# The delta rule's block inverse in quarters of 32 columns instead of halves of 64

## The chip, the cores and the metric

One core of one Trainium2 chip runs the kernel. The metric is the device time of one execution in microseconds (us); lower is better. The kernel before has a median of 1058.83 us over three runs (1057.62 to 1060.48).

## The reference, cut to what matters

Two blocks of two layers each work on 256 rows of 1024 features, in float32. Block one has a gated delta rule of 8 heads beside an attention; its core is a unit lower triangular system for each chunk of the sequence:

```
lower = where(strict, (kb @ k.T) * decay, 0)
tmat  = eye + lower
u     = triangular_solve(tmat, v * beta)
w     = triangular_solve(tmat, kb * exp(gc))
```

The kernel takes chunks of 128 rows, works out the inverse of `tmat` explicitly, and multiplies by it. Block two (four attention branches, gated and merged) is not touched but for the order of its steps.

## The kernel before, in words

**Bulk work.** All projections stream their weights from HBM in units of 512 KB or less: SP issues a unit's load into one of five `raw` slots, ACT rounds it to `w_hi`, which has three slots (`split`, line 1362, through the helper on line 1347), POOL subtracts to get `w_lo` (lines 866 and 868), and TensorE multiplies hi by hi, hi by lo and lo by hi (lines 926, 934 and 941). These units are the `m` steps of the order, their loads and splits the `s` steps.

**Order.** Every engine walks one list, `PLAN`, and executes those of its steps that it has a handler for. The list comes from a string, `ORDER`: each letter takes the next step of its lane (`a` is the delta rule's chain of block one, `b` the attention, `m` the bulk matmuls, `s` loads and splits, and so on). So the string alone sets what stands before what in each engine's queue. Steps signal one another by semaphores. Chain steps on TensorE write the two `chain` buffers in PSUM in turn (`take`, line 951).

**The inverse.** It is done four times: two layers by two groups of four heads, each time for 8 matrices of 128 by 128 at once (4 heads by 2 row tiles). `sub` (DVE, line 1956) solves the 8 by 8 diagonal blocks and spreads them into `xth`, the transposed inverse: each partition holds the 64 columns of its own diagonal half, so that 8 matrices take 512 columns. `x1` (TensorE line 1055, drained by ACT line 1517) turns it into `xh`. Then four levels double the block size, 8 to 16, 32, 64 and 128. Of a level, `invY` multiplies the lower triangle's block with X (TensorE) and masks the product (DVE, line 1999), `invZ` multiplies by X from the other side, once for X and once for its transpose (TensorE, lines 1091 and 1092), and DVE subtracts the two (`invZ` line 2006, `invX` lines 2015 to 2019). On the first three levels and in `x1` each matmul takes a 64 by 64 block on one diagonal half of the array, and the two halves of a matrix follow one another (`half_blocks`, line 965; its matmul is line 970). The fourth level (lines 1080 and 1095) has 64 by 64 blocks that sit on one half only. Each float32 matmul is executed as two passes, so 16 matmuls are 32 records in the trace.

The order of the chain is written in `gdn_chain` (line 235): `sub`, `x1`, then `invY`, `invZ`, `invX` by level, with `vT` after the first level and `kT` in the last, then `kq`, `u`, `st`, `ks`, `o`.

Of the kernel before, what the change touches and what calls it, by code (L numbers as in the profile page):

```python
# [54 lines left out]
K_ID, K_TRIU, K_LEVEL, K_BLOCK, K_NEG, K_STR, K_NSTR, K_TRIL, K_ONE, K_FREQ, K_UNIT, K_LATER, K_HALF, K_OWN = (  # L55
    0, 128, 256, 448, 576, 832, 1088, 1344, 1472, 1600, 1640, 1648, 1776, 1777)
K_COLS = K_OWN + HALF


def shape_constants():  # L60
# [5 lines left out]
    own = HALF * (p // HALF) + f[:, 0:HALF]  # L66
    for n, s in enumerate(LEVELS[:-1]):
        c[:, K_LEVEL + n * HALF:K_LEVEL + (n + 1) * HALF] = (
            (p // (2 * s) == own // (2 * s)) & (p // s % 2 == 1) & (own // s % 2 == 0))
    c[:, K_BLOCK:K_BLOCK + P] = p // BLK == f // BLK  # L70
    c[:, K_OWN:K_OWN + HALF] = p // BLK == own // BLK
    c[:, K_UNIT:K_UNIT + BLK] = p % BLK == np.arange(BLK)[None, :]
    c[:, K_NEG + P:K_NEG + 2 * P] = np.where(f > p, np.float32(NEG), np.float32(0))
    c[:, K_STR:K_STR + P] = p < f
    c[:, K_STR + P:K_STR + 2 * P] = 1
# [159 lines left out]
def gdn_chain(g):  # L235
# [63 lines left out]
def lanes():  # L299
# [20 lines left out]
    "aaaaasammssvamsmssaamaaasaacsccasscccssammcmmsmaacssmmaacssccsmmmamaaasasmdabsmaaabssmmcsmaammassdbm"  # L320
    "adbmssaaammsssammsbadamsabaamamsaaaamssacmasccmaamasbsbbmacccscmammssmsccsaacbcmmbssmambbsaaasssammb"
    "bdsaaaamsssdmmmmaassdwbbssmmmsamcbmmamssssbbdbbmmaaambabxxsasbmaabbbsddmxssbaamswwamaaamaassmamsdwaa"
    "mwbasxsxmmsdmsaxbmwxsaxxxbmbbmxaxvsvsssmssmmmammsmaammsdsaaammsssssvammmmaaaascasscmmsccasscmcassccm"
    "msmaammcmsacsmcasmsassdaaaammasassmmaambbsmambacmaaamdassmssbdbssmaamabammaaamssaaadmsscamacsmssssaa"
    "mmamccacccmssbbscbcmmcamssacammbbsssmabbsmaaamdssaaaammssdsammadmmaabbscbbbmaswmmssdsbbbaassmsssmaaw"
    "maabmmbambsbxmxxbmssdbbbmmsssdamawammaasaadswwmbamasxxbsamaamssbaxdbbwxsxxmmmxxxsssssvsmmsvasadmmmmm"
    "mmsaaaasassaassmmdsssssdssbsdsbbmmmmmmsmmmmammmmsssaassdaasmmbbsaadbbsmmmbsaaasmmbddabbmbbmssaaamvba"
    "bmbsssddmmbbadmmsssybbmbssbmaambdsymsbamdsyyavbymbysydvvmmyssdmvssvvvvdmsvvvdmmmmssdymmmmmmvvvssssss"
    "yvvsmmmmmmmvmmmvsseeessvvvvaeeessmmaaammmbmmmmmmssdmssssssssdmmmmmadsasmsbaaammmbbbaassdasssdbbmbmma"
    "asaamsbmbsddbmbbmaaabmsssvbbmbasmmsabbdmbddsssasmabbssmymmambayddssmbsmbdsssydvyysmsdbsyyvvmmydmmmmv"  # L330
    "svsmdvvvvmsvvyssssmmvvvmmyvvmvvmssemmmmmsseemmvvvveemmme"
# [136 lines left out]
def build(nc, t, out):  # L468
    ctx = ExitStack()
    with ctx:  # L470
# [68 lines left out]
        xh, yh, xth = xx8[:, :, 0:HALF], yy8[:, :, 0:HALF], yy8[:, :, HALF:P]  # L539
        rhs = xx[:, 0, :, :].rearrange("p j n -> p (j n)")  # L540
# [335 lines left out]
        def _(pe):  # L876
            def handlers(p):
# [95 lines left out]

                def memT(r):
# [94 lines left out]
                def invY(g, n):  # L1069
# [6 lines left out]
                    if n < len(LEVELS) - 1:  # L1076
# [7 lines left out]
                def invZ(g, n):  # L1084
# [5 lines left out]
                    if n < len(LEVELS) - 1:  # L1090
# [242 lines left out]
        def _(act):  # L1333
# [15 lines left out]
            def handlers(p):  # L1349
# [167 lines left out]
                def x1(g):  # L1517
                    act.wait_ge(*p.after("tensor", "x1", g))
                    A(xh, heads(half("x1", g)[:, 0:R * 4 * HALF], R * 4), ACT.Copy).then_inc(p.done("x1"), 1)
# [121 lines left out]
                def ln_s(r):  # L1641
                    if r == 0:
# [6 lines left out]
                            stat=stat, avT=avT_, rn=rn, dec_b=dec_b, x1=x1, u=u_, st=st_, onorm_a=onorm_a, onorm=onorm, kinorm=kinorm, iT=iT,  # L1649
# [817 lines left out]
```

## Time and profile before

| | |
|---|---|
| median of 3 runs | 1058.83 us (1057.62 to 1060.48) |
| span of the profiled execution, first to last instruction | 1056.6 us |
| its own time | not listed apart from the span; the median is 2.2 us above the span |
| TensorE busy | 1025.6 us, 97% |
| DVE, ACT, POOL busy | 57%, 55%, 67% |
| granted TensorE clock, mean | 0.997 of full speed |

Busy time of TensorE is that in which at least one matmul is in flight. The chain that ended last says which engine the end of the execution hangs on from one moment to the next. A row of the timeline or of the chain of waits stands for a run of like instructions: its start, the time it takes, and how many there are.

### The profile page before, as it was taken

To read this page: it belongs to the slowest core of one execution; us is meant where nothing else is said; L and a number is where in the kernel's file an instruction comes from. 1 tells how busy PE (TensorE), PEld (TensorE's weight loads), DVE (VectorE), ACT (ScalarE), POOL (GpSimd) and SP (SyncE) were. 2 spreads that over 40 slices of the span, in tenths; PEclk is the share of its full clock that TensorE was granted. 3 is DMA by queue.
4 is the path that set the end of the run, shared out by engine and by line. 5 is a ranking of instruction groups with operands and counts; after the bars stand their busy time and mean duration, and the time that the engine had idled before them with its cause. 6 is when DMAs were issued, how large, how long until landed. Compare 5 with 4: busy or idle time off the path is not lost.

```text
span 1056.6 us, 18561 instructions
## 1 busy us (share of the span) xinstructions
PE 1025.6 (97%) x7112; PEld 886.4 (84%) x7112; DVE 599.0 (57%) x1181; ACT 577.4 (55%) x968; POOL 712.2 (67%) x550
## 2 busy tenths in 40 slices
PE   8999999999999999999999998999999989999986
PEld 8988998888877988899888887788888768888875
DVE  4774366786565557246584563517446560646564
ACT  4754347656644574336656744445576534567652
POOL 4786537872648787556766645897366978744794
PEclk9999999999999999999999999999999999999999
DMA  8664434653425555435444332665233546423451
GB/s 294 192 179 122 139 101 131 173 156 107 134 100 153 180 165 157 140 84 157 141 139 141 115 125 87 209 191 158 81 113 120 186 140 216 133 91 108 140 183 57
DMA packets 80584, 151.59 MB, mean 143 GB/s; under 512 B 6448, under 2 KB 12400, under 8 KB 80496
## 3 DMA queue, kind: packets, MB, share of 16 engines
q1 hardware_dynamic: 80496, 150.41, 46.9%
q8 instruction: 57, 0.93, 0.4%
q14 instruction: 31, 0.25, 0.1%
HBM read 149.34 MB, written 1.05 MB: 142 GB/s over the span
## 4 chain that ended last, share of the span: by engine, by line
PE 88%; DVE 4%; ACT 3%; POOL 3%; issue 2%; DMA 0%; POOLq 0%; SPq 0%; DVEq 0%; ACTq 0%
PE bulk L941 53%; PE bulk L926 12%; PE chain L962 5%; PE chain L970 4%; PE chain L1039 4%; PE chain L1307 1%; PE bulk L934 1%; PE chain L1288 1%; ACT arena L1347 1%; PE chain L1163 1%; PE chain L1179 1%; POOL w_lo L868 1%; DVE arena L1846 1%; PE chain L1030 1%; POOL w_lo L866 1%
## 5 line engine op out<-in xcount | busy, mean ns | idle before, releaser
L866 POOL TENSOR_TENSOR w_lo<-raw,w_hi 128x512 fp32r<-128x512 f32 (+3 forms) x259 | 340.7, 1316 | 292.4 <-ACT w_hi L1347 291.8
L868 POOL TENSOR_TENSOR w_lo<-raw,w_hi 128x512 fp32r<-128x512 f32 (+3 forms) x277 | 375.6, 1357 | 31.8 <-ACT w_hi L1347 31.8
L1347 ACT ACTIVATE w_hi<-raw 128x1024 fp32r<-128x1024 f32 (+4 forms) x277 | 277.3, 1019 | 210.1 <-PE bulk L941 163.4
L941 PE MATMUL bulk<-w_hi,hT_hi 128*128 128x512 f32 (+1 forms) x756 | 306.0, 405 | 0.8 <-ACT arena L1347 0.5
L941 PE MATMUL bulk<-w_hi,hT_lo 128*128 128x512 f32 (+1 forms) x756 | 294.4, 389 | 0.0
L941 PE MATMUL bulk<-w_lo,hT_hi 128*128 128x512 f32 (+1 forms) x756 | 204.2, 389 | 1.9 <-POOL w_lo L868 1.9
L941 PEld LDWEIGHTS bulk<-w_hi,hT_hi 128*128 128x128 f32 x756 | 142.4, 188 | 33.5 <-issue 1.9
L941 PEld LDWEIGHTS bulk<-w_lo,hT_hi 128*128 128x128 f32 x756 | 141.7, 188 | 32.7 <-POOL w_lo L868 3.4
L941 PEld LDWEIGHTS bulk<-w_hi,hT_lo 128*128 128x128 f32 x756 | 142.5, 188 | 26.8 <-issue 1.0
L926 PE MATMUL bulk<-hT_hi,w_hi 128*128 128x256 f32 x384 | 96.3, 289 | 0.0
L926 PE MATMUL bulk<-hT_lo,w_hi 128*128 128x256 f32 x384 | 94.0, 282 | 0.0
L962 PE MATMUL chain<-cst,arena 128*128 128x128 f32 (+1 forms) x544 | 73.4, 276 | 7.8 <-DVE arena L2223 3.5
L962 PEld LDWEIGHTS chain<-cst,arena 128*128 128x128 f32 (+1 forms) x544 | 62.7, 142 | 15.1 <-issue 9.3
L926 PEld LDWEIGHTS bulk<-hT_hi,w_hi 128*128 128x128 f32 x384 | 73.4, 191 | 0.9 <-ACT w_hi L1347 0.7
L1347 ACT ACTIVATE arena<-chain 128x512 f32<-128x512 f32 (+4 forms) x64 | 45.5, 727 | 52.0 <-PE chain L962 23.6
L926 PEld LDWEIGHTS bulk<-hT_lo,w_hi 128*128 128x128 f32 x384 | 73.5, 191 | 0.0
L1846 DVE SCALAR_TENSOR_TENSOR arena<-bulk,par,arena 128x253 f32<-128x253 f32 (+2 forms) x144 | 59.4, 475 | 21.0 <-ACT arena L1347 19.0
L1342 ACT ACT_TABLE_LOAD x44 | 56.5, 1283 | 26.5 <-PE bulk L941 14.3
L1347 ACT ACTIVATE arena<-bulk 128x1024 f32<-128x1024 f32 (+2 forms) x50 | 50.1, 1006 | 17.3 <-PE bulk L941 17.2
L926 PE MATMUL bulk<-hT_hi,w_lo 128*128 128x256 f32 x384 | 53.9, 283 | 0.0
L1347 ACT ACTIVATE arena<-arena,tiny 128x256 f32<-128x256 f32 (+1 forms) x80 | 36.2, 454 | 27.0 <-DVE tiny L2345 19.4
L926 PEld LDWEIGHTS bulk<-hT_hi,w_lo 128*128 128x128 f32 x384 | 49.5, 192 | 0.0
(262 smaller groups left out, 1393.4 us busy)
## 6 DMA issues: line engine op xcount, KB each, us to landing
raw<-in_w_in_dram SPq DMA_DIRECT2D x194, 512.0 KB, 3.6
raw<-in_w_out_dram SPq DMA_DIRECT2D x32, 512.0 KB, 3.7
raw<-in_w_branch_dram SPq DMA_DIRECT2D x16, 512.0 KB, 3.7
raw<-in_w_mem_kv_dram SPq DMA_DIRECT2D x8, 512.0 KB, 3.4
raw<-in_w_merge_up_dram SPq DMA_DIRECT2D x16, 256.0 KB, 2.9
raw<-in_w_in_dram SPq DMA_DIRECT2D x8, 420.0 KB, 3.4
gain<-in_ln_rows_dram SPq DMA_DIRECT2D x4, 512.0 KB, 5.3
gain<-in_gains_dram SPq DMA_DIRECT2D x3, 512.0 KB, 6.1
```

The source lines that it names most:

```text
L866: pool.tensor_tensor(lo_of(p, u)[:, 0:at], raw_of(p, u)[:, 0:at], hi_of(p, u)[:, 0:at].bitcast(F32), ALU.subtract).then_inc(first_part, 1)
L868: pool.tensor_tensor(lo_of(p, u)[:, at:n], raw_of(p, u)[:, at:n], hi_of(p, u)[:, at:n].bitcast(F32), ALU.subtract).then_inc(p.done("split" ...
L926: m = pe.matmul(dst, part[:, k, j * P:(j + 1) * P], b[:, kk, :], start=(not low and kk == 0 and i == 0 and j % 2 == 0), stop=(low and kk = ...
L934: m = pe.matmul(pair[0:n, 0:S], part[:, k, :], b[:, kk, :], start=(not low and kk == 0 and i == 0), stop=(low and kk == tot - 1))
L941: m = pe.matmul(dst, a, part[:, k, :], start=(first and not low and k == 0 and i == 0), stop=(last and low and k == nk - 1))
L962: m = pe.transpose(c[0:n, i * P:i * P + v.shape[0]], v, ident[0:v.shape[0], 0:v.shape[0]])
L970: m = pe.matmul(c[at, col + j * HALF:col + (j + 1) * HALF], a, b, start=(j == 0), stop=(j == R * 4 - 1), skip_group_check=True)
L1030: pe.matmul(c[:, j * P:(j + 1) * P], spread(4 * r + j, 8), rows_T[0:8, :], start=(j == 0), stop=(j == 3), skip_group_check=True)
L1039: m = pe.matmul(c[:, j * P:(j + 1) * P], a, b, start=(j == 0), stop=(j == 3), skip_group_check=True)
L1342: act.preload_act_table_set(sets[func])
L1347: return act.activation(dst, src, func, **more)
L1846: ins = STT(cv[:, j, back:S], b[:, j * S:(j + 1) * S - back], par1[:, p.l, c:c + 1], cv[:, j, back:S], ALU.mult, ALU.add)
```

## The change

The first two levels and `x1` hold 32 by 32 blocks: X in `xq` (columns 64 to 95 of `xx`), its transpose in `xtq` (columns 96 to 127), Y in `yq`. TensorE multiplies them in four diagonal quarters of the array, one matmul for each quarter of a matrix (`quad_blocks`), so twice as many matmuls as before with half the rows, weight columns and moving columns each. DVE and ACT handle 256 columns instead of 512 on these steps. `sub` spreads its blocks in one instruction instead of eight. Before the third level the 32 column form has to become the 64 column form: a new ACT step `x2`, after `invX` of the first level, copies `xq` and `xtq` into `xh` and `xth` in four instructions of 256 columns, each multiplied by a 0/1 factor of the partition, and on the second level DVE's subtraction is done by `apart`, two instructions of 256 columns with a factor of -1 or 0 of the partition in place of one of 512. The table of constants shrinks from 1841 to 1493 columns. `ORDER` is a new string of 1160 letters instead of 1156 (four `x2` steps more), different from the 9th letter on.

```
+QUAD = P // 4
+def level_mask(n):
+    return (K_LEVEL + n * QUAD, QUAD) if n < 2 else (K_LEVEL + 2 * QUAD, HALF)
...
         if n == 0:
+            out.append(("x2", g))
+        if n == 0:
             out.append(("vT", g))
...
 ORDER = (
...
+        quads = [slice(q * QUAD, (q + 1) * QUAD) for q in range(4)]
+        xq, xtq, yq = xx8[:, :, HALF:HALF + QUAD], xx8[:, :, HALF + QUAD:P], yy8[:, :, 0:QUAD]
...
+                def quad_blocks(c, pair, col=0):
+                    for j in range(R * 4):
+                        for at in quads:
+                            a, b = pair(j, at)
+                            m = pe.matmul(c[at, col + j * QUAD:col + (j + 1) * QUAD], a, b, start=(j == 0), stop=(j == R * 4 - 1),
+                                          skip_group_check=True)
+                    return m
...
-                    half_blocks(c, lambda j, at: (xth[at, j, :], ident[at, at])).then_inc(p.done("x1"), 1)
+                    quad_blocks(c, lambda j, at: (xtq[at, j, :], ident[at, at])).then_inc(p.done("x1"), 1)
...
-                    if n < len(LEVELS) - 1:
+                    if n < 2:
+                        quad_blocks(c, lambda j, at: (lt8[at, j, at], xq[at, j, :])).then_inc(p.done("invY"), 1)
+                    elif n < len(LEVELS) - 1:
...
-                    if n < len(LEVELS) - 1:
+                    if n < 2:
+                        quad_blocks(c, lambda j, at: (xtq[at, j, :], yq[at, j, :]))
+                        quad_blocks(c, lambda j, at: (yq[at, j, :], xtq[at, j, :]), 512).then_inc(p.done("invZ"), 1)
+                    elif n < len(LEVELS) - 1:
...
+                def x2(g):
+                    act.wait_ge(*p.after("vector", "invX", g, 0))
+                    for to, of in ((xh, xq), (xth, xtq)):
+                        for n in range(2):
+                            ins = A(to[:, :, n * QUAD:(n + 1) * QUAD], of, ACT.Copy, scale=cst[:, K_PART + n:K_PART + n + 1])
+                    ins.then_inc(p.done("x2"), 1)
...
-                    for r in range(R):
-                        for j in range(4):
-                            ins = TT(xth[:, 4 * r + j, :].rearrange("p (b i) -> p b i", i=BLK),
-                                     over(inv[:, 4 * r + j, :], HALF // BLK), blocks, ALU.mult)
+                    ins = TT(xtq.rearrange("p m (b i) -> p m b i", i=BLK),
+                             inv[:, :, :].unsqueeze(2).broadcast_to([P, R * 4, QUAD // BLK, BLK]),
+                             blocks.unsqueeze(1).broadcast_to([P, R * 4, QUAD // BLK, BLK]), ALU.mult)
...
+                def apart(to, c):
+                    for k in range(2):
+                        x = to[:, :, k * QUAD:(k + 1) * QUAD]
+                        ins = STT(x, c, cst[:, K_PART + 2 + k:K_PART + 3 + k], x, ALU.mult, ALU.add)
+                    return ins
...
+                        if n == 0:
+                            TT(xq, xq, c, ALU.subtract).then_inc(p.done("invZ"), 1)
+                        else:
+                            v.wait_ge(*p.after("scalar", "x2", g))
+                            apart(xh, c).then_inc(p.done("invZ"), 1)
```

What the new string does around the inverse is seen by walking the lanes. This is the stretch of layer 0, group 0 from `rep` to `u` (M with a tile's name is one bulk unit on TensorE, a point is one load and split; the first digit behind a step is the group, the second the level):

```
old: rep sub Mqa0 Mqa0 x1 . . drain_s rope_i Mqa0 invY00 drain_s iT0 Mqa0 . . invZ00 invX00 vT0 Mqa1 Mqa1 . . .
     invY01 Mqa1 Mqa1 . iT1 invZ01 drain_s invX01 Mc01 . invY02 raw00 invZ02 invX02 Mc01 invY03 Mc01 . kT0 invZ03
     kq00 kq01 Mc01 . . u00
new: rep Mqa1 Mqa1 sub x1 rope_i Mqa1 . iT0 Mqa1 . invY00 iT1 invZ00 drain_s invX00 x2 vT0 .
     invY01 Mc01 . invZ01 drain_s invX01 raw00 Mc01 . invY02 raw10 invZ02 Mc01 . invX02 invY03 raw11 kT0 . Mc01 invZ03
     kq00 . kq01 Mc11 u00
```

In layer 1, group 0, the new string has `invY00 iT0 invZ00` as well, with no bulk unit between, and `invZ00 vT0 invY01`. In group 1 of both layers at least eight other matmul passes of 128 columns (`pv`, `pT`, or one or more bulk units) stand between any two steps of the inverse that depend on each other.

## Rows read from the trace of the kernel before

**Rows 1.** The page: busy time, share of the span and instructions of each engine.

```profile
PE 1025.6 (97%) x7112; PEld 886.4 (84%) x7112; DVE 599.0 (57%) x1181; ACT 577.4 (55%) x968; POOL 712.2 (67%) x550
```

**Rows 2.** The page: the chain that ended last, share of the span by engine.

```profile
PE 88%; DVE 4%; ACT 3%; POOL 3%; issue 2%; DMA 0%; POOLq 0%; SPq 0%; DVEq 0%; ACTq 0%
```

**Rows 3.** Waits of TensorE: for whom, us in total, times, longest.

```profile
PE chain L962 <- DVE arena L2223: 3.5, 2, 2.9
PE chain L1179 <- DVE arena L2052: 2.9, 2, 1.4
...
PE bulk L941 <- POOL w_lo L868: 1.9, 3, 0.7
...
PE bulk L941 <- ACT arena L1347: 0.7, 2, 0.5
```

**Rows 4.** Busy time by stretch, the four inversions: length, PE, PEld, DVE, ACT, POOL.

```profile
87.00:132.00 45.00, 44.98 (x555) 39.41 (x553) 16.69 (x41) 16.96 (x20) 27.16 (x22) 1.00 0.45 130
230.00:275.00 45.00, 45.00 (x477) 38.48 (x476) 28.98 (x50) 27.95 (x68) 19.18 (x15) 1.00 0.38 120
420.00:470.00 50.00, 50.00 (x583) 44.88 (x582) 21.53 (x48) 19.47 (x27) 26.60 (x22) 1.00 0.40 117
545.00:610.00 65.00, 65.00 (x565) 55.16 (x564) 39.49 (x71) 40.50 (x79) 44.16 (x34) 1.00 0.47 137
```

**Rows 5.** Groups of TensorE by shape: count, busy us, mean ns of one.

```profile
L970 PE MATMUL chain<-arena 64*64 64x64 f32 x1152 | 38.8, 220 | 0.0
...
L970 PE MATMUL chain<-cst,arena 64*64 64x64 f32 x128 | 4.6, 221 | 0.0
```

**Rows 6.** Timeline of TensorE, single steps: start, us, instructions.

```profile
87.75 1.15 PE L970 MATMUL chain<-cst,arena 64*64 64x64 f32 x32
...
96.29 2.08 PE L970 MATMUL chain<-arena 64*64 64x64 f32 x64
...
124.51 1.11 PE L1080 MATMUL chain<-arena 64*64 64x64 f32 x16
```

**Rows 7.** The chain that ended last, 63 to 65 us: `dec`, two passes by turns.

```profile
63.87 0.11 PE chain L1030
63.97 0.01 PE chain L1032
63.98 0.11 PE chain L1030
64.09 0.01 PE chain L1032
```

**Rows 8.** The same chain at 613 us: a bulk unit, eight passes of 128 columns.

```profile
613.01 2.78 PE bulk L941 x12
615.79 0.89 PE chain L1039 x8
```

**Rows 9.** Groups of DVE by shape: count, busy us, mean ns of one.

```profile
L1846 DVE SCALAR_TENSOR_TENSOR arena<-bulk,par,arena 128x255 f32<-128x255 f32 x48 | 19.9, 476 | 0.4
...
L1999 DVE TENSOR_TENSOR arena<-chain,cst 128x512 f32<-128x512 f32 x12 | 8.3, 692 | 26.4 <-PE chain L970 26.3
...
L1973 DVE TENSOR_TENSOR arena<-tiny,cst 128x64 f32<-128x64 f32 x32 | 7.2, 293 | 0.1
...
L2353 DVE TENSOR_TENSOR arena<-chain,tiny 128x256 f32<-128x256 f32 x12 | 5.1, 424 | 0.4
```

**Rows 10.** Groups of ACT by shape: count, busy us, mean ns of one.

```profile
L1347 ACT ACTIVATE arena<-bulk,par 128x256 f32<-128x256 f32 x48 | 18.8, 474 | 9.1 <-PE bulk L926 9.0
L1347 ACT ACTIVATE arena<-chain 128x512 f32<-128x512 f32 x30 | 17.8, 594 | 42.8 <-PE chain L1039 22.6 <-PE chain L962 14.5 <-PE chain L970 5.7
```

**Rows 11.** Timeline of layer 0, group 0, first level: `invY`, transposes, DVE's mask.

```profile
91.77 1.15 PE L970 MATMUL chain<-arena 64*64 64x64 f32 x32
...
92.85 0.77 PE L962 MATMUL chain<-cst,arena 128*128 128x128 f32 x5
...
93.04 0.69 DVE L1999 TENSOR_TENSOR arena<-chain,cst 128x512 f32<-128x512 f32 x1 [2.74 <-PE chain L970]
```

More of the change, by code:

```diff
@@ L65, in shape_constants @@
     c[:, K_TRIU:K_TRIU + P] = p <= f
[L66 removed]
     for n, s in enumerate(LEVELS[:-1]):
[L68 to L69 removed]
+        at, w = level_mask(n)
+        own = w * (p // w) + f[:, 0:w]
+        c[:, at:at + w] = (p // (2 * s) == own // (2 * s)) & (p // s % 2 == 1) & (own // s % 2 == 0)
+    own = QUAD * (p // QUAD) + f[:, 0:QUAD]
     c[:, K_BLOCK:K_BLOCK + P] = p // BLK == f // BLK
[L71 removed]
+    c[:, K_OWN:K_OWN + QUAD] = p // BLK == own // BLK
+    for n, sign in enumerate((1, 1, -1, -1)):
+        c[:, K_PART + n] = sign * (p[:, 0] // QUAD % 2 == n % 2)
     c[:, K_UNIT:K_UNIT + BLK] = p % BLK == np.arange(BLK)[None, :]
     c[:, K_NEG + P:K_NEG + 2 * P] = np.where(f > p, np.float32(NEG), np.float32(0))
[L74 to L75 removed]
     c[:, K_NSTR:K_NSTR + P] = np.where(p < f, np.float32(0), np.float32(NEG))
@@ L1518, in x1 @@
                     act.wait_ge(*p.after("tensor", "x1", g))
-                    A(xh, heads(half("x1", g)[:, 0:R * 4 * HALF], R * 4), ACT.Copy).then_inc(p.done("x1"), 1)
+                    A(xq, heads(half("x1", g)[:, 0:R * 4 * QUAD], R * 4), ACT.Copy).then_inc(p.done("x1"), 1)
+                def x2(g):
[4 more added lines that the diff above has]
+                    ins.then_inc(p.done("x2"), 1)
                 def half(*key):
@@ L1993, in invY @@
                     v.wait_ge(*p.after("tensor", "invY", g, n))
+                    if n < 2:
+                        at, w = level_mask(n)
+                        TT(yq, heads(half("invY", g, n)[:, 0:R * 4 * w], R * 4), over(cst[:, at:at + w], R * 4),
+                           ALU.mult).then_inc(p.done("invY"), 1)
+                        v.wait_ge(*p.here("invY"))
+                        return None
                     c, up = heads(half("invY", g, n)[:, 0:R * 4 * HALF], R * 4), halves[1]
@@ L1997, in invY @@
                     else:
-                        m = cst[:, K_LEVEL + n * HALF:K_LEVEL + (n + 1) * HALF]
-                        TT(yh, c, over(m, R * 4), ALU.mult).then_inc(p.done("invY"), 1)
+                        at, w = level_mask(n)
+                        TT(yh, c, over(cst[:, at:at + w], R * 4), ALU.mult).then_inc(p.done("invY"), 1)
                     v.wait_ge(*p.here("invY"))
+                def apart(to, c):
[3 more added lines that the diff above has]
+                    return ins
                 def invZ(g, n):
                     v.wait_ge(*p.after("tensor", "invZ", g, n))
+                    if n < 2:
+                        c = heads(half("invZ", g, n)[:, 0:R * 4 * QUAD], R * 4)
+                        if n == 0:
[3 more added lines that the diff above has]
+                            apart(xh, c).then_inc(p.done("invZ"), 1)
+                        v.wait_ge(*p.here("invZ"))
+                        return None
                     c, (low, up) = heads(half("invZ", g, n)[:, 0:R * 4 * HALF], R * 4), halves
@@ L2012, in invX @@
                 def invX(g, n):
+                    if n < 2:
+                        c = heads(half("invZ", g, n)[:, 512:512 + R * 4 * QUAD], R * 4)
+                        if n == 0:
+                            TT(xtq, xtq, c, ALU.subtract).then_inc(p.done("invX"), 1)
+                        else:
+                            apart(xth, c).then_inc(p.done("invX"), 1)
+                        v.wait_ge(*p.here("invX"))
+                        return None
                     c = heads(half("invZ", g, n)[:, 512:512 + R * 4 * HALF], R * 4)
```

35 lines of the change are left out of this document (18 added, 17 removed).

## The prediction

> **What bounds the kernel now.** I read the page first. TensorE is busy 97% of the span and no other engine over 67% [rows 1], and the chain that ended last runs 88% of its length on TensorE [rows 2]. The waits of TensorE say whether that busy time is real work: its longest entry is 3.5 us over two occurrences, and those for split weights are 1.9 and 0.7 us [rows 3]. In the four stretches that hold the inversions TensorE is busy for all but 0.02 us of 205 us, while DVE, ACT and POOL are busy for 68% at most [rows 4]. So in these stretches the chain of the inverse is hidden behind bulk matmuls; what it costs is the TensorE time of its own passes. Time taken off those passes comes off the end, as long as the chain stays hidden; time taken off DVE or ACT does not.
>
> Of that TensorE time the half blocks take 1152 and 128 records, 38.8 and 4.6 us of busy time [rows 5]. Each of the four inversions has ten blocks of 32 records: one for `x1`, one for `invY` and two for `invZ` on each of three levels. The change touches seven of the ten (`x1`, and three on each of the first two levels), 28 blocks in all.
>
> **The change, part by part.** *The passes on TensorE.* A run of 32 records takes 1.15 us and one of 64 takes 2.08 us [rows 6], so 32 more cost 0.93 us, which is 29.1 ns a record or 58.1 ns for a pair of halves; the rest, 0.22 us, is start and tail, and stays with every step. Is a pair as slow as its halves one after the other? The fourth level has the same 64 by 64 blocks on one half only: 16 records take 1.11 us; less 0.22 that is 55.6 ns each [rows 6]. So two halves cost what one costs, though both write the same bank. The chain of waits shows how: in `dec`, whose passes take the lower and the upper rows by turns, the second of a pair starts 0.01 us after the first and the next pair 0.11 us later [rows 7]. A pair's price is thus set by its columns: 0.89 us for eight passes of 128 [rows 8] is 111 ns, against 58.1 at 64. A line through the two has 0.83 ns a column and 5.2 ns fixed; at 32 columns it gives 31.6 ns for a set of four quarters, if the four run beside each other as the two do. A block still has 16 sets (8 matrices, 2 passes). It costs 16 x 31.6 = 0.51 us in place of 16 x 58.1 = 0.93: 0.42 us less, times 28 is **11.9 us less**.
>
> No row shows four quarters together, so bounds. With no fixed part a set is 29.1 ns, and the gain 0.465 x 28 = 13.0 us. If the 0.01 us between the starts [rows 7] is taken at its printed value, four starts are 40 ns, and the gain is 16 x 18.1 ns x 28 = 8.1 us. I take 11.9, from columns, since every run above goes by its columns. Losses are among the rivals.
>
> The Trainium skill, page "TensorE: Matmul & The Clock Gate", section "Wait — 56ns, not 53.3ns?", speaks against the change: from start to start never less than about 25 ns, however few the columns. An estimate by it as a limit on the whole engine is 64 records x 25 ns = 1.6 us a block, 0.67 more than now, and +18.8 us for 28. The starts 0.01 us apart [rows 7] disagree with it as a limit on the engine; as one on each quarter by itself it lies below 31.6 ns and changes nothing.
>
> *DVE.* Masks and subtractions of the first level fall from 0.69 us to about 0.42, by the nearest row of 256 columns, as does the second level's mask; its two subtractions become two instructions of about 0.48 each in place of one of 0.69; the eight instructions of `sub`, 0.29 each, become one of 0.4 to 1.1 [rows 9]. Some 2 us less in each inversion, hidden behind bulk: price 0, at worst what the covers below are short of.
>
> *ACT.* `x1`'s drain shrinks from 0.59 us; `x2` adds four instructions of 256 columns, 4 x 0.47 = 1.9 us, by the nearest row [rows 10], so about 6.6 us over the kernel for an engine at 55%. It stands between the first level's `invX` and the second's last subtraction, beside `invY`, at least a bulk unit or its like (2.8 us [rows 8]) and `invZ` on TensorE. In the same queue stand the splits: a split behind `x2` is 1.9 us later, and POOL after it. TensorE now waits 0.7 and 1.9 us for these in the whole kernel [rows 3], with three units split ahead. Price 0; if the cover is gone, 1.9 us an inversion.
>
> *The order.* The new string puts the first level close together. In layer 0 and layer 1, group 0, only five transposes stand between `invY` and `invZ` of the first level, 0.11 us apart by the passes above, 0.55 us. The mask starts 0.12 us after `invY`'s modelled end (91.77 + 1.15 to 93.04) [rows 11], takes 0.42, and I give the signal back another 0.1: 0.64, plus the 0.07 by which the transposes overlap the tail (92.85 against 92.92). Each place is short by 0.1 to 0.2 us. `vT`, eight transposes or 0.9 us, just covers the subtraction. A third place, `st` to `ks` in layer 0, group 0, keeps 0.9 us of its 2.9 for a drain of 0.59. Together I put 1.0 us on such places, between 0 and 2. What the rest of the string does, loads, splits and POOL's parts included, is not to be read from it: at the layers' ends, where TensorE waits for `mix` and `o`, one wait is worth 1.4 to 2.9 us [rows 3], so I bound it at 4 us either way and take 0. The smaller table of constants is loaded early; no row shows TensorE waiting for that part.
>
> **Sum.** -11.9 + 1.0 = -10.9 us. The profiled execution spans 1056.6 us and would span 1045.7; the median lies 2.2 us above that span, for what lies around it and the spread of the runs, and I keep this distance: **1047.9 us**.
>
> **Rivals.** *Passes are issued at a fixed spacing* (slower). Inside `quad_blocks`, records may follow each other no closer than the 29.1 ns that they average now. Then 64 take 1.86 us, 0.93 more a block, +26.1 us: 1058.8 + 26.1 + 1.0 = 1086. It decides from the point where a record costs over half of 29.1 ns. For it: no row has more than two parts of the array at work. Against it: the 0.01 us between starts [rows 7]. 6%. The rule of the Trainium skill above would make it 1058.8 + 18.8 + 1.0 = 1079, an estimate by that page.
>
> *Only two quarters run together.* A set is 63.2 ns in place of 58.1: +2.3 us, and with the covers 1062. Nothing speaks for it but the missing row. 5%.
>
> *The order takes the gain back.* `x2` comes late behind a split or drain in ACT's queue, the second level's subtraction waits, DVE stands behind it, and TensorE runs out of cover in all four inversions: 4 x 1.9 = 7.6 us, 1055.5. For it: covers of one bulk unit are now the rule there. Against: ACT is idle for 38 to 62% of each stretch [rows 4]. 12%.
>
> *The time is not TensorE's to give.* Weights come no faster, and the 12 us turn up as waits for `w_hi` and `w_lo`: about 1058, no change. Against: POOL is busy for 43 to 68% of the stretches of the inversions [rows 4], and its waits are small [rows 3]. 4%.
>
> **How the numbers follow.** The forecast has the remaining 73%, 1047.9. Its own range is 13.0 + 4 = 17 us to 8.1 - 2 - 4 = 2 us of gain at the extremes, and 1042 to 1053 for most of it. To hold 8 in 10 I reach to the third rival and a little below the first: 1041 to 1056. A measurement here can tell 0.3%, 3.2 us, from no change, so faster means under 1055.6: 0.73 and half of the third rival, 0.79. Same: the other half and the fourth, 0.10. Slower: the first two, 0.11.
>
> **What would show it.** In the profile after: `quad_blocks` with 1792 records of 32 by 32 that take 0.7 us for a run of 64 and 1.2 us for 128 (0.51 and 1.01 with start and tail), in place of 1.15 and 2.08; 384 records left at `half_blocks`; TensorE's busy time 12 us lower, its idle time as before; `x2`'s four instructions near 0.47 us each with nobody waiting for them; DVE's rows of 256 columns at 0.42; a short wait of TensorE for the mask in group 0 of each layer. A run of 64 that takes over 1.15 us, or as many new idle microseconds on TensorE as busy ones gone, would make the prediction wrong.

## The result, and the profile after

The changed kernel takes 1076.78 us, the median of four runs (1073.83 to 1078.76), against 1059.65 for the kernel before, run beside it (1057.62 to 1061.85): a ratio of 1.0141 [1.0104, 1.0178]. It is slower; 1047.9 us was forecast, in a range of 1041 to 1056. Its profiled execution took 1075.3 us.

The head of the page of the kernel after (span; busy time by engine; the chain that ended last, share by engine), against [rows 1, 2]:

```profile
span 1073.5 us, 20351 instructions
...
PE 1022.9 (95%) x8008; PEld 879.9 (82%) x8008; DVE 601.2 (56%) x1161; ACT 582.6 (54%) x984; POOL 713.6 (66%) x550
...
PE 82%; DVE 10%; issue 3%; ACT 3%; POOL 1%; DMA 1%; SPq 0%; DVEq 0%; ACTq 0%; POOLq 0%
```

TensorE's busy time fell by only 2.7 us and its idle time rose from 31.0 to 50.6 us (span less busy time). The chain stands on DVE for 10% of its length, where it was 4%, and the instruction count is not the reason: DVE executes 20 instructions fewer.

The waits of TensorE after (for whom: us in total, times, longest), against [rows 3]:

```profile
PE bulk L953 <- issue: 5.6, 4, 2.6
PE chain L991 <- issue: 4.6, 2, 2.7
PE chain L974 <- DVE arena L2286: 4.4, 1, 4.4
PE bulk L953 <- DVE arena L1855: 3.6, 1, 3.6
PE chain L974 <- DVE arena L2099: 3.4, 1, 3.4
```

Three of these hang on DVE at the ends of the two layers of block one and of block two's last layer (L2286 is `mix`, L2099 the drain `ks`, L1855 `drain_v`, a product of the merge that empties a `bulk` accumulator). One is new in kind: 4.6 us in which the quarter passes (L991) wait for nothing that the profile shows.

The passes themselves did what was forecast. The groups of L991 (quarters, with a constant operand in `x1`) and of L982 (the halves that are left) by form, busy time and mean of one:

```profile
L991 PE MATMUL chain<-arena 32*32 32x32 f32 x1536 | 17.1, 195 | 4.6 <-issue 4.6
L982 PE MATMUL chain<-arena 64*64 64x64 f32 x384 | 12.9, 220 | 0.0
...
L991 PE MATMUL chain<-cst,arena 32*32 32x32 f32 x256 | 3.0, 194 | 0.0
```

Together they are busy for 33.0 us, 10.4 less than the 43.4 of [rows 5]. TensorE's timeline of the first level in layer 0, group 0 (start, us, what, how many):

```profile
107.67 0.75 PE L991 MATMUL chain<-arena 32*32 32x32 f32 x64
108.35 0.76 PE L974 MATMUL chain<-cst,arena 128*128 128x128 f32 x5
109.11 1.28 PE L991 MATMUL chain<-arena 32*32 32x32 f32 x128
110.32 1.09 PE L974 MATMUL chain<-cst,arena 128*128 128x128 f32 x8
111.43 0.64 PE L991 MATMUL chain<-arena 32*32 32x32 f32 x51
114.78 0.32 PE L991 MATMUL chain<-arena 32*32 32x32 f32 x13 [2.71 <-issue]
115.02 0.38 PE L938 MATMUL bulk<-hT_hi,w_hi 128*128 128x256 f32 x1
...
117.06 0.41 PE L938 MATMUL bulk<-hT_hi,w_hi 128*128 128x256 f32 x1
117.28 0.41 PE L938 MATMUL bulk<-hT_lo,w_hi 128*128 128x256 f32 x1
```

A run of 64 takes 0.75 us and one of 128 takes 1.28, where [rows 6] had 1.15 and 2.08. The fifth line is something else: in the middle of one block of 64 passes TensorE stops for 2.7 us. The bulk passes behind the stop start 0.21 to 0.22 us apart; the clock says why. Windows of the kernel after (the stretch and its length; busy us of PE, PEld, DVE, ACT, POOL; the granted clock, where 0.50 is 1.2 GHz and 1.00 is 2.4; DMA share and GB/s):

```profile
112.00:115.00 3.00, 0.29 (x22) 0.21 (x13) 0.81 (x2) 3.00 (x6) 0.80 (x1) 1.00 0.14 48
115.40:118.80 3.40, 3.40 (x19) 3.40 (x18) 0.24 (x1) 0.52 (x1) 3.40 (x4) 0.50 0.30 51
119.00:125.00 6.00, 6.00 (x176) 5.57 (x174) 3.49 (x9) 1.97 (x2) 1.07 (x2) 1.00 0.42 139
```

So a stop of TensorE can be paid twice, first as idle time, then as work at 1.2 GHz. Before, one such stretch lay ahead of the last few us (at 643.6 us); after, there are five (at 115.4, 296.3, 443.0, 654.7 and 1040.4 us), each behind an idle stretch of 1.9 to 4.4 us. The span grew by 16.9 us: idle time by 19.6, busy time by -2.7. The blocks of the inverse gave back 10.4 us of busy time, so the other passes are 7.7 us longer. An estimate from the starts of the matmuls, against the median spacing of passes of the same line and shape, puts some 7 us of that inside the stretches at 1.2 GHz.

The loss builds up in places. Start of the same bulk unit against the kernel before, in us (from the starts of the matmuls in the traces; the kernels of the columns to the right are told below):

```
bulk unit at, in before    after   h_new   n_pool  q_best  q_warm
 194 us (layer 0)           +2.2    +1.7    +2.5    -2.0    -2.1
 377 us (layer 1 starts)   +10.3   +14.3    +5.7    -3.2    -2.4
 680 us (behind block one) +13.8   +19.0    +2.8    -5.5    -7.6
1037 us (last units)       +17.6   +24.5    +8.1    -2.1    -7.2
```

### The profile page after: what moved, and what is told of

It reads as the page before. It is cut to its first block, busy times and chain, and to the rows that moved or that the text cites. A ratio compares the mean times of both kernels' runs of the same rounds, so it can differ in the third digit from the quotient of the medians.

```text
span 1073.5 us, 20351 instructions
## 1 busy us (share of the span) xinstructions
PE 1022.9 (95%) x8008; PEld 879.9 (82%) x8008; DVE 601.2 (56%) x1161; ACT 582.6 (54%) x984; POOL 713.6 (66%) x550
## 4 chain that ended last, share of the span: by engine, by line
PE 82%; DVE 10%; issue 3%; ACT 3%; POOL 1%; DMA 1%; SPq 0%; DVEq 0%; ACTq 0%; POOLq 0%
PE bulk L953 49%; PE bulk L938 12%; PE chain L974 6%; PE chain L1060 3%; PE chain L1333 2%; PE chain L991 2%; DVE arena L2270 2%; PE chain L1314 1%; PE bulk L946 1%; ACT arena L1373 1%; PE chain L982 1%; POOL w_lo L880 1%; POOL w_lo L878 1%; PE chain L1205 1%; PE chain L1051 1%
## 5 line engine op out<-in xcount | busy, mean ns | idle before, releaser
L1373 ACT ACTIVATE w_hi<-raw 128x1024 fp32r<-128x1024 f32 (+4 forms) x277 | 278.5, 1018 | 188.5 <-PE bulk L953 159.5
L953 PE MATMUL bulk<-w_hi,hT_hi 128*128 128x512 f32 (+1 forms) x756 | 306.6, 406 | 3.6 <-issue 1.6
L953 PE MATMUL bulk<-w_hi,hT_lo 128*128 128x512 f32 (+1 forms) x756 | 295.5, 391 | 0.0
L953 PE MATMUL bulk<-w_lo,hT_hi 128*128 128x512 f32 (+1 forms) x756 | 204.2, 389 | 0.8 <-POOL w_lo L880 0.5
L953 PEld LDWEIGHTS bulk<-w_hi,hT_hi 128*128 128x128 f32 x756 | 143.1, 189 | 37.8 <-issue 4.4
L953 PEld LDWEIGHTS bulk<-w_lo,hT_hi 128*128 128x128 f32 x756 | 141.5, 188 | 31.7 <-POOL w_lo L880 2.8
L953 PEld LDWEIGHTS bulk<-w_hi,hT_lo 128*128 128x128 f32 x756 | 143.2, 189 | 27.2 <-issue 1.0
L1373 ACT ACTIVATE arena<-chain 128x1024 f32<-128x1024 f32 (+5 forms) x64 | 44.8, 713 | 79.3 <-PE chain L974 37.8
L1373 ACT ACTIVATE arena<-bulk 128x1024 f32<-128x1024 f32 (+2 forms) x50 | 49.8, 1003 | 14.2 <-PE bulk L953 14.0
L953 PE MATMUL bulk<-w_hi,sT_hi 128*128 128x512 f32 (+1 forms) x108 | 44.6, 413 | 6.2 <-DVE arena L1855 3.6
```

What stands on the lines that cost most here:

```text
L953: m = pe.matmul(dst, a, part[:, k, :], start=(first and not low and k == 0 and i == 0), stop=(last and low and k == nk - 1))
L1373: return act.activation(dst, src, func, **more)
```

## The experiments

### Passes and order taken apart

Two kernels cross the two parts. q_old has the quarters and the old string, with `x2` right behind `invX` of the first level; h_new has the old halves and the new string without its four `x2`.

```
q_old:  new functions;  ORDER = old string + x2 behind each invX(g, 0)
h_new:  old functions;  ORDER = new string - 4 x2
```

Expected of q_old: 

> The quarters with the order of before: each x2 is put right behind the first level's invX, all else stands in the old order. Theory (the re-merged order is at fault: it puts the quarter blocks so close that TensorE runs out of instructions and cover, idles, and the granted clock drops to half behind the idle): without it the quarters' saving of about 10 us shows, 1047 to 1053 us, no TensorE wait for issue of over 1 us in the quarter blocks, no half-clock stretch in block one. Rival 1 (the quarters themselves cost: their dense instructions starve TensorE or let the clock fall wherever they stand): 1062 us or more, with issue waits in the quarter blocks and half-clock stretches behind them.

Expected of h_new: 

> The kernel before (halves of 64 columns, no x2) with the new order, its four x2 letters taken out. Theory: slower than before by what the order costs without the dense instructions: 1068 to 1080 us, with no issue wait in the half blocks of over 1 us. Rival 1: within 3 us of before, 1057 to 1063 us.

q_old: 1059.24 us, ratio 0.9988 [0.9965, 1.0011]. h_new: 1083.47 us, 1.0216 [1.019, 1.0241]. Both miss their ranges: q_old is 6 us above what the theory expected of it, though not as slow as its rival, and h_new 3.5 us. The order by itself costs some 23 us (0.0216 x 1060). Under the new order the quarters take 0.0075 of the time away, 8 us (1.0216 to 1.0141). So the passes are not what makes the kernel slower. Yet with the old order they bring nothing. Waits of TensorE in q_old, then ACT's timeline there ([idle before <- releaser]):

```profile
PE bulk L953 <- ACT w_hi L1373: 3.7, 1, 3.7
```

```profile
424.35 1.70 ACT L1373 ACTIVATE arena<-arena,cst 128x256 f32<-128x256 f32 x4 [6.03 <-DVE arena L2071]
425.96 1.00 ACT L1373 ACTIVATE arena<-bulk 128x1024 f32<-128x1024 f32 x1
426.86 2.94 ACT L1373 ACTIVATE w_hi<-raw 128x1024 fp32r<-128x1024 f32 x3
```

`x2` (L1373, four instructions, 1.70 us) stands at the head of ACT's queue and holds it for 6.03 us, until DVE has done `invX` (L2071). The drain and the splits stand behind it. TensorE waits 3.7 us for the first of these splits, and continues at 1.2 GHz; in q_late, below, where `x2` stands later, this wait is gone.

### `x2` put where ACT need not wait

q_late moves `x2` behind `invY` of the second level (in layer 1, group 0 behind the next bulk unit as well). q_best does the same, except in layer 1, group 1, where `x2` stands behind the first bulk unit that follows `invX` and ahead of three splits.

```
-         if n == 0: out.append(("x2", g))
+         if n == 1: out.append(("x2", g))     # behind invY of that level; q_best: not for (g, l) = (1, 1)
```

Expected of q_late: 

> The quarters with the order of before, x2 put behind the second level's invY (in layer 1, group 0 behind the bulk unit after it) instead of right behind the first level's invX. Theory (with the old order the quarters' gain was eaten by x2: it stood at the head of ACT's queue for 6 us until invX came, the splits behind it came 3.7 us late to TensorE, and the clock fell to half behind that wait): the wait of 3.7 us and the half-clock stretch of 6.8 us in layer 1 are gone, and the time is 1049 to 1053 us. Rival (the passes of the quarters don't save what their busy time says): 1057 to 1060 us, as with the early x2.

Expected of q_best: 

> The quarters with the order of before; x2 behind the second level's invY as in q_late, but in layer 1, group 1 it stands ahead of the three splits that follow the first bulk unit after invX, since there those splits held x2 up until 567 us and DVE and TensorE with it. Theory: the wait of 4.7 us in layer 1, group 1 and the half-clock stretch of 6.8 us behind it go, the lead of 6 us that q_late had over before at 566 us stays to the end: 1051 to 1056 us. Rival (some other wait takes their place, so that the quarters are worth nothing in this kernel): 1058 to 1063 us.

q_late: 1062.66 us, 1.0031 [1.0007, 1.0055], a miss. It was 6.1 us ahead of before at 566 us and lost it there, by the timeline (ACT, DVE and TensorE rows):

```profile
566.99 1.69 ACT L1373 ACTIVATE arena<-arena,cst 128x256 f32<-128x256 f32 x4
568.80 1.79 DVE L2045 SCALAR_TENSOR_TENSOR arena<-chain,cst,arena 128x256 f32<-128x256 f32 x4 [11.66 <-ACT arena L1373]
...
570.65 1.11 PE L974 MATMUL chain<-cst,arena 128*128 128x128 f32 x4 [4.72 <-DVE arena L2045]
```

In layer 1, group 1 `x2` now stood behind splits whose slots come free only when TensorE has gone on; `apart` (L2045) sat 11.66 us, and TensorE 4.72. q_best mends this one place: 1053.97 us, **0.9921 [0.989, 0.9952]**. By their place in an in-order queue these few instructions of ACT cost 7 us (0.9988 against 0.9921, times 1060) or 12 (1.0031).

### Which block's order

```
q_new1: quarters; block one in the new order, block two in the old
q_new2: quarters; block one in the old order (as q_old), block two in the new
```

Expected of q_new1: 

> The quarters, with the steps of block one in the new order and those of block two in the old. Theory: the loss lies in block one and at its end, so 1070 to 1078 us, as the changed kernel. Rival 2 (the new order of block two is what costs): 1048 to 1058 us.

Expected of q_new2: 

> The quarters, with block one in the old order and block two in the new. Theory: 1048 to 1057 us (the new order of block two adds its two waits of 2.6 and 3.6 us for the turned merge, little else). Rival 2: 1065 us or more.

q_new1: 1072.74 us, 1.0116 [1.0097, 1.0135]. q_new2: 1065.86 us, 1.0056 [1.0035, 1.0077], a miss: block two's order costs 0.0068 beside block one's old order (against q_old), 7 us, and 0.0025, 2.7 us, beside its new one, which the intervals alone do not tell from nothing (the last units start 3.3 us earlier in q_new1's profile than in that of the kernel after). The chain of waits of the kernel after shows the last place where it does:

```profile
1037.28 1.03 ACT sT_hi L1373
...
1038.40 0.06 DVE sT_lo L2457
...
1039.55 1.22 DVE arena L1855
...
1040.81 7.14 PE bulk L953 x24
```

The last bulk units stand right behind `gT`'s transposes. Nothing covers the transposes' drain on ACT (`sT_hi`), their subtraction on DVE (`sT_lo`, L2457) and, behind it in DVE's queue, the product of `drain_v` (L1855): 3.6 us in the waits. The 5.6 us of `L953 <- issue` in the waits of the kernel after belong to block two's order too: q_new2 has 5.1 of them, the kernel before 1.9.

### The stop inside a block of passes

All stops inside quarter blocks that the traces show start at the same place of TensorE's instruction stream. Each pass is two instructions there (weights and matmul). From the traces:

```
kernel    instructions of TensorE before the stop -> length of the stop, us
after      1985 -> 2.9     7873 -> 2.1
q_old      1729 -> 1.1    10945 -> 1.6
n_mixb     1729 -> 0.6     1985 -> 2.1    7873 -> 1.5
n_apart    7873 -> 4.0
n_ends     7873 -> 4.2
n_ends2    7873 -> 1.8
n_pool     1729 -> 1.0     1985 -> 2.1    7873 -> 1.8
n_endpool  7873 -> 3.9
q_new1     1729 -> 1.0     1985 -> 1.8    7873 -> 2.1
q_new2     2241 -> 0.2    10945 -> 1.5
q_best     1729 -> 1.0    10945 -> 1.6
q_warm     1729 -> 1.1
q_shift    5057 -> 1.2     7873 -> 0.8
```

All these counts leave 193 when divided by 256. The DMA queue that brings instructions (64 transfers of 16 KB over the run, 57 before) has a transfer that belongs to each stop, and work resumes 2.2 to 3.0 us after its start. For the stop at 111.88 us the transfer starts at 112.48, takes 0.96, and work resumes at 114.78. Where no stop is, the transfer started earlier: q_late, told above, issues the same passes in the same sequence as q_old and has no stop at all in a quarter block; its transfers start 3.6 and 3.2 us ahead of instructions 1729 and 10945, those of q_old 1.2 and 1.1 us ahead. A run of 128 quarter passes uses up 256 instructions in 1.28 us, faster than one such transfer brings the next. To test it, q_shift takes q_late and adds one instruction that waits for two signals long given behind each of 128 early bulk matmuls, so that everything later moves by 128 instructions, half a transfer; what counts is where stops turn up.

```
+                                        if shift[0]:
+                                            shift[0] -= 1
+                                            pe.wait_ge(ident_in, 16)
+                                            pe.wait_ge(x_in, 16 * R)
```

Expected of q_shift: 

> As q_late, with two satisfied waits after each of 128 matmuls of the first bulk tiles, so that about 128 instructions more stand ahead on TensorE's queue and every later instruction moves by half a fetch of 256. Theory (TensorE's gaps inside the quarter blocks lie where a fetch of 256 instructions has to arrive while a run of 128 passes eats 256 instructions in 1.2 us): the gaps move to other passes, at instruction counts of the same remainder by 256, and are fewer or more by chance; time within 3 us of q_late. Rival (the gaps belong to the blocks, by the array or by semaphores): they stay at the same passes.

q_shift: 1062.55 us, 1.0009 [0.9979, 1.0039]. It has two stops, in other blocks of passes than q_old's, at counts with the same remainder. That the passes outrun their instructions is the reading that fits all of these; what sets the start of a transfer stays open, so the stops cannot be foretold from the order. The best kernels keep 1.1 to 2.6 us of them, the kernel after 5.0.

### The two places of layer 0, and both layers' ends

n_mixb takes the kernel after and moves `mix_b` of group 0 in layer 0, eight DVE instructions, behind `ks` and `o` of group 1. n_apart moves one bulk unit from ahead of the first `invY` to behind `vT`.

```
- u10 drain_sg10 zgainzb1 gmulg10 mix_b0 mm68 st1 . mm69 ks1 mm70 . o10
+ u10 drain_sg10 zgainzb1 gmulg10 mm68 st1 . mm69 ks1 mm70 . o10 mix_b0     (n_mixb)
- ... Mqa0 . invY00 iT1 invZ00 drain_s invX00 x2 vT0
+ ... . invY00 iT1 invZ00 drain_s invX00 x2 vT0 Mqa0                        (n_apart)
```

Expected of n_mixb: 

> The changed kernel with one step moved: in layer 0 mix_b of group 0 (eight DVE instructions of 0.6 to 0.8 us) stands behind the DVE parts of ks and o of group 1 instead of ahead of them. Theory (the new order lets DVE's queue hold up the delta rule's chain at layer 0's end): TensorE's wait of 3.4 us for ks and the half-clock stretch behind it go, 1070 to 1074 us. Rival (another wait takes their place): 1075 to 1078 us, as the changed kernel.

Expected of n_apart: 

> The changed kernel with one bulk unit moved, in layer 0, group 0: from ahead of the first level's invY to behind vT, so that it stands between the first level's invZ and the second's invY. Theory (dense quarter blocks in a row run out of fetched instructions): the gap of 2.7 us inside the second level's invY and the half-clock stretch behind it go, 1071 to 1075 us; in layer 1, where nothing moved, both stay. Rival: the gap stays or turns up elsewhere in the same stretch, 1075 to 1078 us.

n_mixb: 1070.75 us, 1.0096 [1.0065, 1.0128]; n_apart: 1072.46 us, 1.0114 [1.0071, 1.0157]. Each time lies in the range expected; in the profiles the wait at 293 us is gone from n_mixb and the stop at 112 us from n_apart, where the stop in layer 1 stays and grows from 2.1 to 4.0 us. The times alone do not show the gains: both intervals overlap with that of the kernel after. n_ends has both, and `mix_b` of group 0 moved in layer 1 too; n_ends2 has block two in the old order besides.

Expected of n_ends: 

> The kernel after, with the two repairs of its order put together and the first one made in layer 1 too: mix_b(0) behind ks and o of group 1 at both layers' ends, and the bulk unit ahead of layer 0's first invY moved behind vT. If the loss of the order lies in these few places, the gains add: 6.0 and 4.3 us as measured one by one, and 4 to 6 us for the wait for ks or mix near 650 us with the half clock behind it, so 1076.8 - 15 = 1060 to 1063. Rival: the places hide one another or move on to the next wait, or the loss lies spread over the order: 1066 to 1070.

Expected of n_ends2: 

> n_ends with block two's steps in the old order. Block two's new order cost 6.6 us beside block one's old one, and 4.0 us beside block one's new one. If the places are independent this is 4 to 7 us under n_ends, 1055 to 1059, within 5 us of the version with the old order and x2 well placed (0.9921 of before). Rival: what block one's order loses lies elsewhere, and this stays above 1062.

n_ends: 1068.41 us, 1.0059 [1.0033, 1.0085], in the rival's range. The two gains add (0.0045 + 0.0027 of 0.0082), but the third place gave nothing: TensorE's wait for `mix` at the end of layer 1 stands as before.

```profile
PE chain L974 <- DVE arena L2286: 4.4, 1, 4.4
```

n_ends2: 1065.07 us, 1.002 [0.9996, 1.0044]. It is 4.1 us under n_ends by the ratios, with overlapping intervals, but above 1062 and 1.0% above q_best: the rival's case, in which what block one's order loses lies elsewhere. Following that wait back led to the next finding.

### DVE beside POOL

The chain of waits of the kernel after, ahead of that wait (start, us, what):

```profile
649.01 6.30 DVE arena L2270 x8
...
655.43 1.24 DVE arena L2286
...
656.80 1.94 PE chain L974 x8
```

L2270 is `mix_b` once more. Eight instructions take 6.3 us; in the chain of the kernel before they take 2.2. The same group in DVE's table of the kernel before (L2207 there), busy us and mean ns:

```profile
L2207 DVE SCALAR_TENSOR_TENSOR arena<-arena,tiny 128x128 f32<-128x128 f32 x32 | 8.8, 346 | 0.4
```

and of the kernel after:

```profile
L2270 DVE SCALAR_TENSOR_TENSOR arena<-arena,tiny 128x128 f32<-128x128 f32 x32 | 23.1, 791 | 0.4
```

The same 32 instructions on the same shapes cost 14.3 us more. By the single records, 14 of them take 1.35 to 1.39 us and the other 18 take 0.34 to 0.35 (the 13 in the expectations below is a miscount); the long ones are those that fall beside POOL. POOL's timeline in the kernel after, at the `mix_b` of 288.77 to 295.06:

```profile
288.94 1.33 POOL L878 TENSOR_TENSOR w_lo<-raw,w_hi 128x512 fp32r<-128x512 f32 x1 [4.18 <-ACT w_hi L1373]
290.22 1.35 POOL L880 TENSOR_TENSOR w_lo<-raw,w_hi 128x512 fp32r<-128x512 f32 x1
291.53 1.33 POOL L878 TENSOR_TENSOR w_lo<-raw,w_hi 128x512 fp32r<-128x512 f32 x1
292.82 1.31 POOL L880 TENSOR_TENSOR w_lo<-raw,w_hi 128x512 fp32r<-128x512 f32 x1
```

Four POOL instructions, and four long ones on DVE (1.385, 1.374, 1.365 and 1.347 us): each instruction of DVE lasts about as long as the subtraction on POOL that it falls beside. All 14 long ones start while a subtraction runs and end 0.15 us behind its end; one that already runs when a subtraction starts keeps its 0.34 to 0.35 us. In the kernel before no `mix_b` instruction is longer than 0.352 us, since POOL rests during all four (one POOL instruction starts 0.05 us before the end of the first). The Trainium skill, page "GPSIMD Engine Reference", section "1. Specifications", states that GpSimd shares its SBUF interfaces with VectorE and contends with VectorE instructions that have two SBUF inputs; `mix_b` has two such inputs, and these rows agree, with the size: 1.0 us an encounter.

n_pool tests it with the order of the kernel after left as it is: POOL alone waits for `mix_b` ahead of the four units that ran beside it. n_endpool adds two such waits to n_ends2. A second profile of h_new's kernel (h_pool) asks whether the pattern repeats.

```
+        POOL_BEHIND = {("one", 0, 71): 0, ("one", 0, 76): 1, ("one", 1, 71): 0, ("one", 1, 76): 1}
...
                     pool.wait_ge(*slot_value(p.sec, p.l, u))
+                    if (p.sec, p.l, u) in POOL_BEHIND:
+                        pool.wait_ge(*p.after("vector", "mix_b", POOL_BEHIND[p.sec, p.l, u]))
```

Expected of n_pool: 

> The kernel after, with one wait more on POOL for each mix_b: the w_lo subtractions of unit 71 start behind mix_b(0), those of unit 76 behind mix_b(1), in both layers. The order is that of after. Theory: the four mix_b take 6.3, 4.2, 6.3 and 6.3 us there because 13 of their 32 DVE instructions take 1.35 to 1.39 us beside a POOL subtraction and the others 0.34 to 0.35; kept apart, each takes 2.2 to 2.4 us, and the three of them that the next layer's or the next step's start hangs on give 4.1 us each on DVE's chain, less where another wait takes over, with the half clock behind the waits at 293 and 652 us gone or shorter: 8 to 14 us off, 1063 to 1069 (1.003 to 1.009 of before). Rival: DVE's order alone sets the waits, or the wait only moves to w_lo, which POOL now delivers 1.4 to 2.2 us later: 1073 to 1077.

Expected of n_endpool: 

> n_ends2 (1.002 of before) with POOL's subtractions of unit 76 behind mix_b(1) in both layers. Its two mix_b(1) take 4.2 and 6.3 us, as 6 of their 16 instructions stand beside POOL; they should take 2.2 to 2.4. In layer 1 the whole 4.1 us lies on the chain to TensorE's wait for mix (4.4 us), with 1.7 us of half clock behind it; in layer 0 mix has slack. So 4 to 6 us off: 0.996 to 0.998 of before. Rival (POOL's lateness takes it back): 1.000 to 1.004.

Expected of h_pool: 

> The kernel of h_new (halves, new order without x2) once more, one look, to see whether the profile of its mix_b repeats: 13 of 32 instructions over 1.27 us, the four groups 6.3, 4.2, 6.3 and 6.3 us; time near 1.0216 of before.

n_pool: 1067.75 us, 1.0049 [1.0024, 1.0074]. Four waits more, and the kernel is 0.92% faster, 9.7 us, with intervals that don't overlap. Its `mix_b` group:

```profile
L2274 DVE SCALAR_TENSOR_TENSOR arena<-arena,tiny 128x128 f32<-128x128 f32 x32 | 8.8, 346 | 0.4
```

and POOL's timeline there, the first line being where POOL was held:

```profile
644.14 2.35 POOL L882 TENSOR_TENSOR w_lo<-raw,w_hi 128x512 fp32r<-128x512 f32 x1 [10.94 <-DVE arena L2274]
646.46 1.29 POOL L884 TENSOR_TENSOR w_lo<-raw,w_hi 128x512 fp32r<-128x512 f32 x1
```

The 14.3 us of DVE are gone, and with them TensorE's waits of 3.4 and 4.4 us and the stretches at 1.2 GHz behind them. No wait for `w_lo` takes their place. Two other stretches at 1.2 GHz appear, at 669.0 and 839.7 us. The first follows a wait of 2.4 us, 1.5 in the kernel after, for the norm between the blocks (L1791). Three of its four DVE instructions take 1.6 to 1.8 us beside POOL, and the fourth 0.75: it is the same meeting at another place. The first line also shows the meeting from POOL's side: the subtraction beside `mix` (which has two inputs in SBUF too) takes 2.35 us in place of 1.3. n_endpool: 1060.48 us, 0.9989 [0.9974, 1.0004], 0.31% or 3.3 us under n_ends2, less than the 4 to 6 us expected and with overlapping intervals; its profile has no long `mix_b` left (all 0.34 to 0.54 us). h_pool, one run: 1080.33 us, and the group again at 23.1 us for 32: the pattern belongs to the order.

### The clock

q_warm is q_best with eight extra passes of the identity ahead of `mT(1)`: in the idle stretch of TensorE at 637 us, and at layer 0's end, where they seem to cost 0.8 us (377 us in the table above).

```
                     c = take("mT", h)
+                    if h:
+                        identity_times(c, 8)
```

Expected of q_warm: 

> As q_best, with eight matmuls of the identity by itself ahead of mT of the second half, at the ends of the layers, where TensorE idles for 1.5 to 3 us before that step; their product is overwritten. Theory (the half-clock stretches follow idle of TensorE): the half-clock stretch at about 645 us goes, and 0.5 to 2 us with it, 1050 to 1055 us. Rival: the clock falls there all the same and the extra passes cost up to 2 us.

q_warm: 1052.61 us, **0.9905 [0.9874, 0.9936]**, the best of all; against q_best's 0.9921 the intervals overlap, so the times alone do not show a gain. The profile does show that the clock was kept. Windows of q_best (an idle stretch, then the next):

```profile
636.00:639.00 3.00, 0.91 (x9) 0.94 (x10) 1.81 (x4) 0.00 (x0) 0.00 (x0) 1.00 0.17 66
639.50:642.80 3.30, 3.30 (x9) 2.59 (x8) 1.23 (x1) 2.67 (x3) 1.44 (x2) 0.50 0.00 0
```

and of q_warm over the same place:

```profile
636.00:646.00 10.00, 9.04 (x46) 7.26 (x45) 2.37 (x2) 4.93 (x5) 5.50 (x5) 1.00 0.16 48
```

In q_warm no stretch at 1.2 GHz is left ahead of the last few us. One at 1022 us, where q_warm changes nothing, is gone too, so part of the difference between the two profiles (2.1 us at 680 us, 5.1 at 1037) is not due to the edit. TensorE idled there for 2.7 us in both, and the clock fell in q_best alone. The two profiles of h_new's kernel show the same: each has an idle stretch of 3.37 us at 297 us, and what follows it is, in h_new and then in h_pool:

```profile
300.60:303.80 3.20, 3.20 (x10) 2.68 (x10) 1.70 (x2) 0.60 (x1) 0.00 (x0) 0.50 0.09 28
...
300.40:303.60 3.20, 3.20 (x18) 2.70 (x18) 1.70 (x2) 0.60 (x1) 0.00 (x0) 1.00 0.06 19
```

One program, one idle stretch, 10 matmuls or 18 in the same time. So whether the clock falls behind a wait is not settled by the wait, and one profile's list of such stretches is one sample.

## Why the prediction was wrong

**The passes were right.** The step "if the four run beside each other as the two do" holds: 64 more passes cost 1.28 - 0.75 = 0.53 us, 33 ns for a set of four, where 31.6 was forecast. A block costs 0.40 us less instead of 0.42, so 28 of them 11.2 instead of 11.9; the busy time fell by 10.4. Rivals one and two fall with it. The Trainium skill, page "TensorE: Matmul & The Clock Gate", section "Wait — 56ns, not 53.3ns?", has starts never closer than about 25 ns; 0.53 us over 64 is 8.3 ns, so for quarters of the array that is no limit on the engine.

**What reaches the end is less, but the same in both orders:** 8 us from h_new to the kernel after, and 8.4 us (1 - 0.9921) from before to q_best. The steps had no term for the stops at instruction transfers, 0 to 5 us a kernel.

**The step that failed is the order: "I bound it at 4 us either way and take 0".** It measured +23 us with halves (h_new), and as much with quarters (1.0141 against 0.9921). I had bounded it by the waits that the kernel before has at its layers' ends, 1.4 to 2.9 us [rows 3]. But these are the waits that the old order leaves: under the new one the same instructions (h_new) leave waits of 4.4, 3.6 and 3.4 us. The sign that the prediction named last came: 19.6 us of new idle time on TensorE against 10.4 of busy time gone from the blocks. Of the 23 us, the experiments place:

- about 10 us: POOL's subtractions beside `mix_b` (n_pool), idle time and clock together, shown clear of the noise;
- about 3 us: the stop in layer 0, with the clock behind it (n_apart), which the profile shows (the unit at 194 us starts 4.0 us earlier, the last units 2.1) and the times alone do not; it lies in quarter passes, so it is part of the order's price with quarters and not with halves;
- 3 to 7 us: block two's steps (7 clear of the noise in q_new2; the 3 to 4 of q_new1 and n_ends2 are not).

Moving `mix_b` (n_mixb) is no fourth term, since it also took `mix_b` away from POOL. Put together in n_endpool the repairs win back 16 of the 23 us (1.0141 to 0.9989). What the other 7 us are was not tested, and the cause of these stays open.

**The steps "DVE: price 0" and "ACT: price 0" were right in size and wrong in kind.** The durations came out as forecast: `apart` 0.48, masks 0.42, `x2` 1.70 us for four. But a price from a row of one engine takes the duration as the instruction's own. DVE's `mix_b`, which the change doesn't touch, went from 0.35 to 0.79 us on average because its neighbour in time changed. The kernel before had a sign of it, in the view of one DVE line (count: ns min/median/max), an instruction on four columns:

```profile
L2345 DVE TENSOR_SCALAR tiny<-tiny x12: 169/170/1214, 749.9 to 973.7; 128x4 f32<-128x4 f32 x12
```

An instruction of 0.17 us that once takes 1.21 was held by something; I read means and medians and passed over the maximum. The trace says by what: the long one at 973.67 us starts while a POOL subtraction runs (973.54 to 974.86) and ends 0.03 us behind it, and the one at 789.94 does likewise. The meeting itself is thus not new. Counted as time above the shortest instruction of the same line and shape, whatever the cause, DVE has 64 us of it in the kernel before and 80 in the kernel after, and `mix_b` has 14.5 of the difference; new is that it lies on a chain that TensorE waits for.

One row was misread without harm: the 0.7 us of [rows 3] that the prediction counts as a wait for split weights is a wait for a drain on ACT (its tile is `arena`, not `w_hi`).

**The third rival** ("the order takes the gain back", 12%) had the right name, the wrong place and a third of the size. Its mechanism, `x2` late in ACT's queue, is not what happened: none of the waits of TensorE shown above leads to it, and in the kernel after `apart` (L2045) idles for TensorE alone. It does occur under the old one (q_old, q_late), where it costs 7 to 12 us, near its 7.6 but in one of the four inversions instead of a quarter in each. The fourth rival, time that is not TensorE's to give, fell with q_best.

## What to carry to other kernels

A new order of steps is a change of its own: time it alone, with the old instructions, before pricing what comes with it. In the trace, look for instructions of one line whose longest is several times their shortest, and see what other engine runs at that moment; where VectorE and GpSimd meet on a chain that matters, one wait on GpSimd can be worth more than the work that was saved. And a copy put into an in-order queue costs what stands behind it while it waits, not what it takes.

## What was not expected of the hardware

- A DVE instruction with two inputs in SBUF that starts while a POOL subtraction runs ends just behind it: the 0.34 us of `mix_b` become 1.35 to 1.39 beside 1.3 us of POOL (kernel after), and POOL's 1.3 becomes 2.35 beside a DVE instruction of 1.23 (n_pool).
- Quarter passes start 8.3 ns apart on average, four to a set of 33 ns, though the four write the same columns of `chain` in PSUM, each on its own partitions.
- Quarter passes stop for 0.2 to 4.2 us, always at counts with the same remainder by 256; that they outrun the supply of instructions is the reading that fits.
- In the kernel after, work at 1.2 GHz followed five idle stretches of TensorE of 1.9 to 4.4 us, and one of 2.55 us (848.5 us) was followed by none; behind the same 3.37 us the clock fell in one profile of h_new's kernel and stayed in the other. The idle time is the larger part of the loss: 19.6 us more of it, against some 7 us for the clock.
